# A rebuilt convolution stage, and half blocks dealt out product by product among row sums and picks

## The reference

```python
qkv_a = causal_dwconv_silu(pad_front(qkv_a), conv_w)       # y[t] = sum of 4 taps, then silu
qa = l2_norm(qa.reshape(B_, Lp, H_A, DK_A)) * (DK_A ** -0.5)
ka = l2_norm(ka.reshape(B_, Lp, H_A, DK_A))
beta = pad_front(jax.nn.sigmoid(b_a))
g = pad_front(-jnp.exp(a_log) * jax.nn.softplus(a_a + dt_bias))
o_a = gated_delta_rule(qa, ka, va, beta, g)[:, PAD:]
o_a = rms_norm_2(o_a, o_norm_a) * jax.nn.silu(z_a...)
log_f = jax.nn.log_sigmoid(f_b + f_bias)
```

## Time and profile before

| | us |
|---|---|
| median of 3 runs | 1991.13 (1989.74 to 2017.59) |
| the profiled execution, its time | 1991.74 |
| its span | 1990.4 |
| PE busy | 1786.6 (90%) |
| DVE, ACT, POOL busy | 1237.7, 705.2, 428.2 |

### The profile page before, as it was taken

The page is one execution under the profiler, slowest core; times in us unless marked ns, Lnnn a source line. Parts: engine busy times, 40 slices in busy tenths (PEclk is TensorE's granted clock), DMA queues, the critical chain, the costliest instruction groups (busy, mean ns, idle before and its releaser), DMA issues. The chain is left out here.

```text
span 1990.4 us, 23779 instructions
## 1 busy us (share of the span) xinstructions
PE 1786.6 (90%) x9472; PEld 1349.0 (68%) x9472; DVE 1237.7 (62%) x2173; ACT 705.2 (35%) x1202; POOL 428.2 (22%) x373
## 2 busy tenths in 40 slices
PE   7989999999999989799998999997888878787878
PEld 6869988877799869778988877894333333333333
DVE  4766645765576447735455545678776677667754
ACT  4545534344355343523352334342222122212211
POOL 0330000400000000003104000024554544454541
PEclk9999999999999989889999999998888988889889
DMA  7334555444455543402221212479999999999995
GB/s 265 107 106 170 180 185 184 157 176 155 169 173 188 190 148 107 148 22 85 86 102 47 86 64 86 152 275 421 421 422 421 422 421 422 421 421 421 421 421 245
DMA packets 62622, 453.57 MB, mean 228 GB/s; under 512 B 6945, under 2 KB 7073, under 8 KB 7857
## 3 DMA queue, kind: packets, MB, share of 16 engines
q0 software_dynamic: 36864, 268.45, 32.4%
q1 hardware_dynamic: 25040, 178.27, 25.2%
q10 hardware_dynamic: 608, 5.34, 0.7%
HBM read 450.98 MB, written 1.05 MB: 227 GB/s over the span
## 5 line engine op out<-in xcount | busy, mean ns | idle before, releaser
L2335 PE MATMUL banks<-uv_rows,diag 128*128 128x512 f32 x1024 | 515.3, 668 | 121.1 <-ACT diag L2384 116.7
L549 DVE TENSOR_TENSOR weights_lo<-weights,weights_hi 128x1024 fp32r<-128x1024 f32 x336 | 419.5, 1290 | 260.8 <-ACT weights_hi L540 260.7
L2335 PEld LDWEIGHTS banks<-uv_rows,diag 128*128 128x128 f32 x1024 | 217.5, 216 | 418.3 <-issue 273.4
L540 ACT ACTIVATE weights_hi<-weights 128x1024 fp32r<-128x1024 f32 x336 | 336.7, 1051 | 391.1 <-PE banks L556 383.2
L554 PE MATMUL banks<-x_hi,weights_hi 128*128 128x256 f32 (+1 forms) x1472 | 425.1, 289 | 7.7 <-DVE weights_lo L549 5.1
L556 PE MATMUL banks<-x_hi,weights_lo 128*128 128x256 f32 (+1 forms) x1472 | 419.3, 285 | 0.0
L555 PE MATMUL banks<-x_lo,weights_hi 128*128 128x256 f32 (+1 forms) x1472 | 418.8, 285 | 0.0
L2471 DVE CUSTOM_DVE_ANT_0 uv_rows<-uv_rows,tokens 128x1024 f32<-128x1024 f32 x256 | 306.3, 1224 | 165.3 <-DMA uv_rows<-expert_uv,index 165.2
L2494 POOL DMA_INDIRECT uv_rows<-expert_uv,index x256 | 307.9, 1203 | 343.2 <-PE banks L2335 287.9
L554 PEld LDWEIGHTS banks<-x_hi,weights_hi 128*128 128x128 f32 x1472 | 280.7, 191 | 15.5 <-issue 7.2
L556 PEld LDWEIGHTS banks<-x_hi,weights_lo 128*128 128x128 f32 x1472 | 280.5, 191 | 0.1
(11 more groups left out here) (378 smaller groups left out, 2243.3 us busy)
## 6 DMA issues: line engine op xcount, KB each, us to landing
weights<-weights SPq DMA_DIRECT2D x168, 1024.0 KB
uv_rows<-expert_uv,index POOLq DMA_INDIRECT x256, 18.4
sb_first<-constants_first ACTq DMA_DIRECT2D x1, 1920.0 KB, 8.5
sb_peer<-constants_peer ACTq DMA_DIRECT2D x1, 1544.0 KB, 6.8
sb_always<-constants_always ACTq DMA_DIRECT2D x1, 1467.0 KB, 14.0
h<-x SPq DMA_DIRECT2D x1, 1024.0 KB, 5.8
out<-h SPq DMA_DIRECT2D x4, 256.0 KB, 4.6
sb_now<-constants_now ACTq DMA_DIRECT2D x1, 216.0 KB, 4.8
```

The source lines that it names most:

```text
L540: self.act.activation(self.w_hi[b % SLOTS][:, f], self.raw[b % SLOTS][:, f], ACT.Copy).then_inc(self.hi_made, 1)
L549: self.dve.tensor_tensor(self.w_lo[b % SLOTS][:, f], self.raw[b % SLOTS][:, f], self.w_hi[b % SLOTS][:, f], ALU.subtract).then_inc(self.lo ...
L2335: mm = pe.matmul(self.bank(2 * t + half), self.diag[:, k, :], self.uv[n % NUV][:, f], start=(u < NT and k == 0), stop=(u >= UNITS - NT and ...
```

## The change

- The small rows' three weight sets are padded to start at columns 0, 32 and 64, and become one set of 24 products with 72 output rows (bank 6). It stands behind the first convolution block. Splitting its weights moves ahead of the input norm.
- The vector work on the small rows is cut in four parts (`scalar_lam`, `vector_lam`), one after each of the convolution blocks 0 to 3. The turned columns come after block 5, the row sums of q and k after blocks 7 and 9.
- ACT makes the last tap from PSUM (an activation with a scale, two for a block), DVE the other three. SiLU and squares follow block by block on ACT, one or more blocks behind. Three pairs of banks take the blocks instead of four.
- The picks after the convolution go in 8 steps of two, and behind each step come three pieces (9 products) of the first three fills, which left points 12, 16 and 18 of the first delta group.
- In the delta rule the fills at points 0 and 1 are dealt out: one piece (three products) behind each of the first three picks, the other five behind the fourth.
- In the outputs stage each row sum is followed by one piece of a fill; the last four fills are dealt out over the 12 pairs of picks, two or three pieces behind each. ACT takes the roots behind the fourth fill instead of the fifth.

```diff
-small = small.reshape(KD, P, 3 * H2).transpose(1, 0, 2).reshape(P, -1)
+small = np.pad(small.reshape(KD, P, 3, H2), ((0, 0), (0, 0), (0, 0), (0, 32 - H2)))
+small = small.reshape(KD, P, 96)[:, :, 0:SMALL_W].transpose(1, 0, 2).reshape(P, -1)
...
+SMALL_W = 64 + H2
+CONV_FILLS = range(0, 3)
-DELTA_POINTS = ([i for i in range(26) if i not in (2, 25)], [0, 1, 3, ...])
+DELTA_POINTS = ([i for i in range(26) if i not in (2, 12, 16, 18, 25)], [0, 1, 3, ...])
...
 def tensor_small(self):
-        for g in range(3):
-            for k in range(KD):
-                mm = self.product(self.bank(4 + g, SM)[0:H2, :], [y[:, k, g * H2:(g + 1) * H2] for y in self.small], ...)
+        for k in range(KD):
+            mm = self.product(self.bank(6, SM)[0:SMALL_W, :], [y[:, k, :] for y in self.small], [y[:, k, :] for y in self.x], ...)
...
 def tensor_conv(self):
+        for s in range(st.n):
+            pe.wait_ge(self.lo_made, PARTS * (b + 1))
+            if s >= 3:
+                pe.wait_ge(self.freed_a.sem, self.freed_a.at("conv", s - 2))
...                                           # the 48 products of block s
+            if s == 0:
+                self.tensor_small()
+            elif s == 5:
+                self.tensor_token_columns()
+            elif s in (7, 9):
...                                           # 8 row sums of q or k
+        pe.wait_ge(self.rms_read.sem, self.rms_read.at("conv", 2))
+        steps = self.fill_steps(CONV_FILLS, 8)
+        for c in range(8):
+            pe.wait_ge(self.rms_ready.sem, self.rms_ready.at("conv", c // 4 + 1))
+            if c < 3:
+                pe.wait_ge(self.freed_a.sem, self.freed_a.at("conv", st.n - 2 + c))
+            else:
+                pe.wait_ge(self.rms_scaled.sem, self.rms_scaled.at("conv", c - 2))
...                                           # two picks
+            for part in steps[c]:
+                self.tensor_fill(*part)
...
 def scalar_conv(self):
+            act.activation(self.conv_in[:, at:at + 2, pad:], self.conv_bank(s), ACT.Copy)
+            for sub in range(2):
+                moved = act.activation(self.conv_out[:, j, :], self.conv_bank(s)[:, sub, :], ACT.Copy, scale=w[:, j, pad:pad + 1])
+            moved.then_inc(self.freed_a.sem, 1)
+            if s < 4:
+                self.scalar_lam(s)
+            for old in behind.get(s, ()):
+                self.scalar_conv_silu(old)
+            if s == 10:
+                act.preload_act_table_set(LN_EXP)
...                                           # wait rms_read, Ln, Exp for q and k
...
 tensor_delta:
             for hh in range(HG):
                 mm = pe.matmul(self.bank(hh, SM), C["pick"][0:H2, h * P:(h + 1) * P], self.row(name), start=True, stop=True)
+                if hh < HG - 1 and (group, j) in FILL_AT:
+                    self.tensor_fill(FILL_AT[group, j], hh, hh + 1)
             mm.then_inc(d["rows"].sem, 1)
-            fill(j)
+            if (group, j) in FILL_AT:
+                self.tensor_fill(FILL_AT[group, j], HG - 1, KD)
...
 tensor_outs:
+            f = next(fills)
             for hd in range(H2):
                 mm = pe.matmul(self.out_sums(i), C["to_row"][:, hd * H2:(hd + 1) * H2], squares[hd], ...)
-            mm.then_inc(self.rms_sums.sem, 1)
-            self.tensor_fill(next(fills))
-        self.tensor_fill(next(fills))
+                if hd == H2 - 1:
+                    mm.then_inc(self.rms_sums.sem, 1)
+                self.tensor_fill(f, hd, hd + 1)
+        steps = self.fill_steps(fills, 12)
...
-            if c in (3, 7, 11):
-                self.tensor_fill(next(fills))
+            for part in steps[c]:
+                self.tensor_fill(*part)
...
 scalar_outs:
-        for _ in range(4):
+        for _ in range(3):
             self.scalar_fill(next(fills))
         act.preload_act_table_set(LN_EXP)
...
+            if c == 2:
+                self.scalar_fill(next(fills))
```

More of the change, by code:

```diff
@@ L1505, in token_scalar @@
         return self.tok[0:TILES[t][1], o:o + 1]
-    def scalar_row_squares(self, name, xs, squares):
-        for x, sq in zip(xs, squares):
-            self.act.activation(sq, x, ACT.Square).then_inc(self.rms_sq.sem, 1)
-    def tensor_row_sums(self, name, squares, width):
-        pe = self.pe
-        for j in range(len(squares)):
-            sums = self.bank(7 - j, width)[0:H2, :]
-            pe.wait_ge(self.rms_sq.sem, self.rms_sq.at(name, j + 1))
-            for k in range(H2):
-                mm = pe.matmul(sums, self.C["to_row"][:, k * H2:(k + 1) * H2], squares[j][:, k, :], start=(k == 0), stop=(k == H2 - 1))
-            mm.then_inc(self.rms_sums.sem, 1)
@@ L1537, in tensor_row_scale @@
-    def tensor_row_scale(self, name, n, width):
-        pe = self.pe
-        for j in range(n):
-            rows = self.lam[:, 9 - j, 0:width]
-            pe.wait_ge(self.rms_ready.sem, self.rms_ready.at(name, j + 1))
-            for half in range(2):
-                if j:
-                    pe.wait_ge(self.rms_scaled.sem, self.rms_scaled.at(name, 2 * (j - 1) + half + 1))
-                for k in range(4 * half, 4 * half + 4):
-                    mm = pe.matmul(self.bank(k, width), self.C["pick"][:, k * P:(k + 1) * P], rows, start=True, stop=True)
-                mm.then_inc(self.rms_rows.sem, 1)
@@ new lines, in tensor_conv @@
+        pe.wait_ge(self.rms_read.sem, self.rms_read.at("conv", 2))
[4 more added lines that the diff above has]
+                pe.wait_ge(self.freed_a.sem, self.freed_a.at("conv", st.n - 2 + c))
+            else:
+                pe.wait_ge(self.rms_scaled.sem, self.rms_scaled.at("conv", c - 2))
+            for j in range(2):
+                hd = 2 * (c % 4) + j
+                mm = pe.matmul(self.bank(2 * (c % 3) + j, SM), self.C["pick"][:, hd * P:(hd + 1) * P], self.row(self.ROOTED[c // 4]),
+                               start=True, stop=True)
+            mm.then_inc(self.rms_rows.sem, 1)
+            for part in steps[c]:
+                self.tensor_fill(*part)
@@ L1593, in scalar_conv, with fill_steps @@
+    def fill_steps(self, fills, n):
+        steps = [(i, k) for i in fills for k in range(KD)]
+        parts = [steps[len(steps) * j // n:len(steps) * (j + 1) // n] for j in range(n)]
+        return [[(i, min(k for f, k in part if f == i), 1 + max(k for f, k in part if f == i)) for i in sorted({f for f, _ in part})]
+                for part in parts]
     def scalar_conv(self):
         act, pad, st = self.act, CONV_K - 1, self.st["conv"]
+        w = self.C["conv"].rearrange("p (c k) -> p c k", k=CONV_K)
+        behind = {4: (0, 1), 5: (2, 3), 6: (4, 5), 7: (6,), 8: (7,), 9: (8,), 10: (9,), 11: (10,)}
+        act.wait_ge(self.conv_moved, 1)
@@ L1620, in vector_conv @@
             value = {}
-            for tap in range(CONV_K):
+            for tap in range(pad):
                 for sub in range(2):
```

266 lines of the change are left out of this document (131 added, 135 removed).

## The result

| | before | changed |
|---|---|---|
| median | 1993.96 us (1989.74 to 2017.59, 4 runs) | 2034.63 us (2030.69 to 2035.18, 4 runs) |
| ratio, 95% interval | | 1.0173 [1.0134, 1.0212] |
| profiled execution: time, span | 1991.74, 1990.4 | 2035.03, 2033.7 |
| mean granted clock | 0.936 | 0.918 |

A forecast was written before the change was run, and what follows sets the result against it. PE bounds the convolution stage, DMA the last 640 us. Gains of 16.2 + 1.8 + 9.3 less 2.1 and 8.7 make 16.5 us: span 1973.9, time 1975, eight-in-ten range 1962 to 1990.

The forecast's parts named there:

- Part 1: From the input norm to the first delta group: 16.2 us gained, delta starting at 849.1 instead of 865.3.
- Part 2: First picks of delta group 1, now at the full clock: 15.5 us instead of 17.3, a gain of 1.8.
- part 4: Dealt fills of delta group 2: 2.1 us lost, from DVE time left bare and six more returns.
- Part 5: Outputs stage: 8.7 us lost, from added returns, a 4.7 us idle ahead of the picks and the fifth fill's move.
- The rival that says the opposite: The clock falls in the dealt stages because picks use 8 of 128 rows: +28 us, time 2003; chance 0.07.
- The return: On PE, going from one kind of product to the other and back: 0.2 us each, 47 added, bounds 0 to 0.3.
- The rival of free returns: Weight loads pulled ahead on PE make all added returns cost nothing: +9.4 us gain, time 1966; chance 0.18.
- Parts 3 and 4: Delta rule: three fills fewer in group 1 gain 9.3 us; dealt fills in group 2 lose 2.1.

The follow-up runs named there:

- E1: Changed kernel with every pick reading 128 rows instead of 8, the added rows zero; 1970.92 us, 0.9849 of before.
- E11: Changed kernel with every pick over 64 rows instead of 8; 2009.48 us, 1.0058 of before.
- E10: E5 with the attention's 16 picks over 128 rows too and ScalarE's roots ahead of the fifth fill's move; 1952.73 us, 0.9780 of before.
- E2: Changed kernel with delta rule and outputs stage as before, only the convolution's picks dealt, 8 rows; 1993.41 us, 0.9978 of before.
- E3: E2 with the three fills of the convolution's picks whole, behind the third, sixth and eighth pair; 1986.06 us, 0.9944 of before.
- E4: Kernel before with only the outputs stage's row sums dealt, one fill piece behind each of 24; 2006.55 us, one run.
- E12: E1 with the weights of the outputs stage's 24 row sums 128 columns wide instead of 8; 1965.62 us, 0.9830 of before.
- E6: Kernel before with only its convolution, delta rule and outputs stage picks over 128 rows; 1984.00 us, 0.9917 of before.
- E5: E3 with all the picks that E1 widened over 128 rows, all fills whole; 1965.07 us, 0.9832 of before.
- E8: Changed kernel with every pick over 32 rows instead of 8; 2022.87 us, 1.0135 of before.

## Why the prediction was wrong, step by step

E1 has the dealing, the waits and the order of the changed kernel and a clock that holds, so it tests the steps; E11 does so for the price of the returns of few-row picks, as its clock held through the picks of the convolution and of both delta groups. Stages in us:

| stage | forecast | changed | E11 | E1 | E10 |
|---|---|---|---|---|---|
| norm to delta | 117.6 | 127.3 | 118.4 | 115.6 | 116.1 |
| delta to products | 15.5 | 26.6 | 17.2 | 14.8 | 13.2 |
| products to outputs | 238.7 | 249.4 | 241.1 | 238.8 | 239.3 |
| outputs to attention | 64.3 | 85.4 | 85.4 | 62.3 | 50.1 |
| attention to experts | 119.0 | 123.0 | 123.9 | 118.7 | 115.4 |

- **The step that failed** is an assumption that stands under parts 1, 2, 4 and 5: the dealt picks run at the full clock. Part 5 said it openly, "the lower clock after such a wait stays as it was: 5.9 us at 0.50"; it was 48.8 us. The rival that says the opposite was written down with its right mechanism and the right place, and was given 0.07. Its price, 28 us, was too low too (and its own terms, 38 us of work at 1.8 times the time, make 30): it left out the first picks of group 1, where the clock cost 9.4 us (26.6 against E11's 17.2), those of group 2 (0.50 to 0.61 between 1015 and 1030), and the attention, into which the low clock runs for 10 us.
- What misled was the one row against it: 14.00 us at 1.00 in which picks and fills took turns of 3.9 and 3.0 us. That row is of a coarser pattern than the one that the change makes, and even the coarser one did not hold the clock in E2, E3 and E4 (0.66, 0.66, 0.67). The rows for the rival, group 1's picks at the lower clock and 5.9 us at 0.50, were both of 8-row picks, and so was about a third of the low clock in the convolution's 0.71; the rest of that lay behind a wait.
- The busy share says nothing here: 48.80 of 48.80 us busy at 0.50. The Trainium skill, "TensorE: Matmul & The Clock Gate", under "What's actually happening", says that the gate is set by how busy PE has lately been. E1 has the changed kernel's instructions with 128 instead of 8 rows; read as the share of time in which PE works, the rule does not give the difference, and the measurement decides.
- *The return* was mis-sized. It was 0.2 from the earlier trace rows, with a high bound of 0.3. Measured at full clock: 0.28 to 0.30 for row sums with 8 columns, 0.39 for picks of 8 rows (2.44 against 2.05), much the same for 32 and 64, nothing behind the first of a row where the f32 weights fill the array (E1, E12). The bound failed because the earlier trace rows has no pick next to a product. E11 against E1 gives its share without the clock: 2.8 and 2.4 us in the first two stages.
- *The rival of free returns* was half right. The Trainium skill, same page, "Step-by-step: what each phase is for", says that a weight load is pulled ahead when it does not conflict with the rows in use or goes to the background buffer. The trace agrees for weights of 128 by 128 and not for smaller ones. With 0.18 it was the second favourite, but for this kernel's shapes it was wrong.
- *Part 1* holds. With 64 rows delta starts 118.4 us after the norm (117.6 forecast). *Part 2*'s terms add up to 15.3 and not to 15.5; E1 has 14.8.
- *Parts 3 and 4* came out right together by luck. The three fills out of group 1, less part 4's loss in group 2, made 7.2 in the forecast and 7.1 in E1 (245.9 to 238.8). But the fills alone, E6 against E5, are worth 7.5 (246.6 to 239.1) and not 9.3, and the loss of 2.1 is not there with full picks (E1 238.8, E5 239.1); with 64 rows it is about 2.3 (E11 241.1).
- *Part 5* holds but for the clock and the price of a return: the idle of 4.7 was 4.63, and ScalarE's rows show no drain at a table load, here or in E10.
- From the forecast's 1973.9 to the span of 2033.7: 3.6 before the norm, 9.7, 11.1, 10.7, 21.1 and 4.0 by stage, less 0.4 behind. Set against E11, the clock is 8.9 and 9.4 of the first two. In the outputs stage, 23.1 us lie between the changed kernel and E1; 12 returns at 0.39 are 4.7 of them by estimate, and the rest is the clock. The 3.6 before the norm are not the change's: TensorE's program is the same there, the changed profile has a granted clock of 0.83 from 380 to 400 us and that of before 1.00, and E10 and E11, with the same start as the changed kernel, have 1.00 there and reach the norm at 729.9 and 730.4.

Left open: why the clock held to 841 and 862 with 8 and 32 rows, and through all the picks with 64, in the convolution stage, where after the idle of the outputs stage none of the three came back; whether columns streamed at few rows count in part or not at all was not separated. Nor was it tried whether a shorter idle ahead of 8-row picks would have let the clock hold there. The low readings that remain in E10 (885 to 895, 1020 to 1030, 1200 to 1215) were not followed.

## What to carry to other kernels

A matmul with few contraction rows (8 and 32 here, and 64 behind an idle stretch) streams in the same time as a full one but did not hold TensorE's clock, and a mix of it with full products ran at 0.50 for 48.8 us while the engine showed 100% busy: pad such operands to 128 rows with zeros, which costs one memset and here gave 64 us to one kernel and some 15 to the other, the cheaper returns included. Mixing full f32 products with others cost 0.3 to 0.4 us for each return where the f32 weights were smaller than 128 by 128; filled up, it was free but for the first of a row. When a forecast leans on the clock of a new pattern, look for a row with the same grain and the same shapes, and if the only favourable one is coarser, give the unfavourable case the larger chance. And a clock reading of one profile is one sample: the same code read 0.85 in one run and 0.66 in others.

## What the runs showed of the hardware that was not expected

- Rows with nothing but zeros in them hold the clock as well as any: E1's picks multiply 120 zero rows and run at 1.00 where the 8-row picks ran at 0.50 to 0.65.
- Few rows read and few rows written are different things: row sums of 8 output rows in steps of three products kept 1.00 for 26.5 us (1143.9 to 1170.4), picks of 8 input rows in as fine a grain did not (0.56 from 862.4 to 889.0).
- Once low, the dealt pattern did not bring the clock back in 48.8 us (49 and 47 us in E11 and E8). Whole fills of 3.0 us between picks brought it back for part of the time (0.66 and 0.70 on average in E3).
- The kernel before was itself spread from 1989 to 2017 us, its version with picks over 128 rows from 1979.65 to 1988.51 (E6, 8 runs).
